# Two chained blocks on one core: norms issued one column block ahead, modulations and weight splits moved forward, and matvec chunks at three per four experts

## What is computed

```python
h = rmsnorm(x, norm1_g) * (1 + sc1) + sh1
z = h @ w_in                    # latents, conv input, gates
x = x + gt1 * ((g_attn * y_attn + g_conv * y_conv) @ w_out)
h = rmsnorm(x, norm2_g) * (1 + sc2) + sh2
x = x + gt2 * hierarchical_moe(h, ...)   # 32 experts, 4 groups of 8, top 1 group, top 2 experts
x = rmsnorm(x, final_norm_g)
# second block, layer 0 (gated delta rule) and layer 1 (softmax attention with forget gates), each:
h = rmsnorm(x, norm_w) * (1 + scale) + shift
x = x + gate * mixer(h)
```

## Time and profile before

| what | value |
|---|---|
| median of 3 runs | 1219.14 us (1217.68 to 1224.91) |
| the profiled execution | 1220.97 us |
| its span, first to last instruction | 1219.2 us |
| mean granted TensorE clock | 0.932 of full |
| PE busy | 1070.9 us, 88% |
| DVE, ACT, POOL busy | 639.4, 491.9, 398.6 us |

### The profile page before, as it was taken

How to read it: one execution, slowest core, us unless ns; L and a number is a source line. 1 busy time by engine, 2 the same in 40 slices (tenths; PEclk the granted TensorE clock), 3 DMA queues, 4 the chain that set the end, 5 groups by cost and what they waited for, 6 DMA issues and landing times.

```text
span 1219.2 us, 20059 instructions
## 1 busy us (share of the span) xinstructions
PE 1070.9 (88%) x8110; PEld 925.1 (76%) x8110; DVE 639.4 (52%) x1382; ACT 491.9 (40%) x1100; POOL 398.6 (33%) x337
## 2 busy tenths in 40 slices
PE   2589778899899999999599989999889977999986
PEld 2487567788777777776588879899779866888865
DVE  7777976374434444545554535544454434455463
ACT  2434334322211011014386756836643533565542
POOL 0551334020000000101477464455433425554431
PEclk9699989799799999999699989999989978999988
DMA  9522451577089999731222222323221213323301
GB/s 349 212 91 109 142 203 35 234 267 297 1 337 353 406 387 400 294 133 74 103 104 97 79 70 71 104 70 106 70 70 39 102 37 123 117 107 113 131 35 35
DMA packets 25724, 186.22 MB, mean 153 GB/s; under 512 B 4128, under 2 KB 4768, under 8 KB 5536
## 3 DMA queue, kind: packets, MB, share of 16 engines
q1 hardware_dynamic: 24048, 184.77, 39.8%
q10 hardware_dynamic: 432, 0.18, 0.1%
q0 software_dynamic: 1152, 0.00, 0.0%
HBM read 196.46 MB, written 1.05 MB: 162 GB/s over the span
## 4 chain that ended last, share of the span: by engine, by line
PE 70%; DVE 18%; ACT 8%; issue 3%; DMA 2%; POOL 1%; DVEq 0%; ACTq 0%; POOLq 0%; SPq 0%
PE bank L666 67%; DVE arena L2092 5%; DVE sz L2092 2%; PE bank L670 2%; DVE arena L2089 2%; ACT wH L1489 1%; DVE hT L2092 1%; ACT arena L1489 1%; ACT xH L1486 1%; DVE wL L2089 1%; ACT arena L1486 1%; DVE xL L2092 1%; DVE arena L2095 1%; ACT tmpc L1486 1%; DMA ring<-in_exw,small 1%
## 5 line engine op out<-in xcount | busy, mean ns | idle before, releaser
L2916 POOL TENSOR_TENSOR wL<-ring,wH 128x512 fp32r<-128x512 f32 x210 | 279.8, 1346 | 336.2 <-ACT wH L1489 335.7
L666 PE MATMUL bank<-xH,wH 128*128 128x256 f32 x800 | 253.7, 317 | 33.5 <-DVE xL L2092 25.6
L666 PE MATMUL bank<-xH,wL 128*128 128x256 f32 x800 | 233.4, 292 | 0.0
L666 PE MATMUL bank<-xL,wH 128*128 128x256 f32 x800 | 232.6, 291 | 0.0
L666 PEld LDWEIGHTS bank<-xH,wH 128*128 128x128 f32 x800 | 160.4, 200 | 49.5 <-issue 34.7
L666 PEld LDWEIGHTS bank<-xH,wL 128*128 128x128 f32 x800 | 161.2, 201 | 4.7 <-issue 4.3
L1489 ACT ACTIVATE wH<-ring 128x512 fp32r<-128x512 f32 x264 | 154.0, 619 | 21.5 <-DMA ring<-in_wts 12.9
L666 PEld LDWEIGHTS bank<-xL,wH 128*128 128x128 f32 x800 | 160.4, 200 | 0.0
L666 PE MATMUL bank<-ring,xg 128*128 128x256 f32 x640 | 145.3, 380 | 2.6 <-DMA ring<-in_exw,small 1.5
L666 PEld LDWEIGHTS bank<-ring,xg 128*128 128x128 f32 x640 | 119.8, 190 | 24.5 <-issue 6.0
L2092 DVE SCALAR_TENSOR_TENSOR sz<-ring,cact,sz 128x512 f32<-128x512 f32 x168 | 132.1, 786 | 5.0 <-DMA ring<-in_wts 0.3
(11 more groups left out here) (201 smaller groups left out, 1831.7 us busy)
## 6 DMA issues: line engine op xcount, KB each, us to landing
ring<-in_wts SPq DMA_DIRECT2D x123, 1024.0 KB, 4.9
ring<-in_exw SPq DMA_DIRECT2D x32, 1536.0 KB, 8.9
ring<-in_wts SPq DMA_DIRECT2D x1, 1152.0 KB, 5.3
xT<-in_xT SPq DMA_DIRECT2D x1, 1024.0 KB, 13.5
out<-hT SPq DMA_DIRECT2D x4, 256.0 KB, 2.5
cst<-in_cst SPq DMA_DIRECT2D x1, 928.5 KB, 11.7
ring<-in_wts SPq DMA_DIRECT2D x1, 640.0 KB, 3.5
vec<-in_vec SPq DMA_DIRECT2D x1, 216.5 KB, 5.5
```

The costliest lines, as they stand in the source:

```text
L666: return pe.matmul(o, l, r, start=start, stop=stop, skip_group_check=True)
L2916: return pool.tensor_tensor(o, x, h.bitcast(F32), ALU.subtract)
```

## The change

It does five things. (1) In norms 0, 2 and 3 DVE issues y one block ahead: y0, y1, l0, y2, l1, ..., y7, l6, l7; ACT and POOL keep their order. (2) `modulation(2)` moves into the expert loop at u = 30, `modulation(3)` in front of the third output projection; each waits for the last y of the norm before. (3) The splits of `gqk0a` and `gqk0b` move into the loop: ACT does two quarters at each of u = 38 to 41, DVE four turns at each of u = 40 and 41 (its own quarters are the fourth of each chunk; at u = 41 they stand behind `low_y(4)`), POOL does them when its loads are out. ACT's wait becomes: the last expert and the last matvec chunk that lie in columns 12288 to 20480, which are `ov3` and `ada2_1_4a`. (4) `fqk0b`'s splits move into norm 3, one quarter behind every second block, on ACT, DVE and POOL. (5) Matvec halves are placed at three per four experts, the last two at u = 34, and matvec steps run at 8 in 5 iterations. The ring gets fixed spots for `ov1`, `ov4`, `ov6`, and `before()` no longer stops at the first chunk that covers the start.

```diff
-        while h < 28 and 10 * h <= 7 * u:
+        while h < 28 and (4 * h <= 3 * u or u == 34):
@@ ring_spots
         k = PLACE[name][1]
+        at = {"ov1": 0, "ov4": RING, "ov6": 4096}.get(name, at)
@@ before
             out.append(ORDER[m])
-            if a <= lo:
-                break
@@
+AHEAD = [(0, "y")] + [(k + x, n) for k in range(8) for x, n in ((1, "y"), (0, "l")) if k + x < 8]
@@ the expert loops of PE and DVE
-                for _ in range((u + 1) * 7 // 5 - u * 7 // 5):
+                for _ in range((u + 1) * 8 // 5 - u * 8 // 5):
                     next(gad, None)
@@ ACT, high()
                         if name[:4] == "gqk0":
-                            e.wait_ge(dn_p, 39)
-                            e.wait_ge(ada_acc, (23, 7))
+                            for s, key in under_split():
+                                e.wait_ge(s, key)
@@ ACT, normed (POOL's normed alike)
                     fn(oh[:, k, :], hT[:, k, :], ACT.Identity, bias=shift(k)).then_inc(norm_a.up((u, k)))
+                    if u == 3 and k % 2:
+                        split.go()
@@ ACT, expert loop
+                if 38 <= u:
+                    split.go()
+                    split.go()
...
-            split.need("gqk0b")
@@ DVE
             def modulation(u, at, out_of, *gains):
                 e.wait_ge(ada_out, out_of)
+                if u:
+                    e.wait_ge(norm_d, (u - 1, 7, "y"))
...
             def normed(u, r, oh, ol, shift):
-                for k in range(8):
-                    stt(hT[:, k, :], xT[:, k, :], modA[:, k:k + 1], r, ALU.mult, ALU.mult).then_inc(norm_d.up((u, k, "y")))
-                    e.wait_ge(norm_a, (u, k))
-                    stt(ol[:, k, :], hT[:, k, :], shift(k), oh[:, k, :].bitcast(F32), ALU.add, ALU.subtract).then_inc(norm_d.up((u, k, "l")))
+                for k, n in AHEAD:
+                    if n == "y":
+                        stt(hT[:, k, :], xT[:, k, :], modA[:, k:k + 1], r, ALU.mult, ALU.mult).then_inc(norm_d.up((u, k, "y")))
+                    else:
+                        e.wait_ge(norm_a, (u, k))
+                        stt(ol[:, k, :], hT[:, k, :], shift(k), oh[:, k, :].bitcast(F32), ALU.add, ALU.subtract
+                            ).then_inc(norm_d.up((u, k, "l")))
+                        if u == 3 and k % 2:
+                            split.go()
@@ DVE, expert loop
+                if u == 30:
+                    modulation(2, 56, 15, vcol("norm_w_2", 0, 8), vcol("final_norm_g", 0, 8))
                 if 2 <= u and (u - 2) % 8 == 7:
                     low_y((u - 2) // 8)
+                if 40 <= u:
+                    for _ in range(4):
+                        split.go()
...
-            split.need("gqk0b")
-
-            modulation(2, 56, 15, vcol("norm_w_2", 0, 8), vcol("final_norm_g", 0, 8))
...
+            modulation(3, 80, 23, vcol("norm_w_2", 8, 8))
             nx = out_proj("ao", 2, 3, 64)
...
-            split.need("fqk0b")
-            modulation(3, 80, 23, vcol("norm_w_2", 8, 8))
+            split.need("fqk0a")
```

More of the change, by code:

```diff
@@ L471, in build_program @@
         r2_d = sig("r2_d", range(3))
-        norm_d = sig("norm_d", [(u, k, n) for u in G4 for k in K8 for n in ("y" if u == 1 else "yl")] + [(4, k, "y") for k in K8])
+        norm_d = sig("norm_d", [(u, k, n) for u in G4 for k, n in ([(k, "y") for k in K8] if u == 1 else AHEAD)] + [(4, k, "y") for k in K8])
         norm_a = sig("norm_a", [(u, k) for u in G4 for k in K8])
@@ L584, in ada_name, with under_split @@
             return f"ada{j}" if j < 12 else f"ada2_{j // 6 - 2}_{j % 6}"
+        def under_split():
+            names = [n for n in WIDE if SPOT[n][0] < RING and 12288 < SPOT[n][1]]
+            return [freed_by([n for n in names if (n[:3] == "ada") == x][-1])[0] for x in (False, True)]
         def used(name):
```

## The result

Slower by 0.6%, where I had forecast a little faster: median 1227.91 us (1222.02 to 1235.07, 9 runs) against 1219.24 (1217.68 to 1224.91, 9 runs), ratio 1.0064 with a 95% interval of 1.0036 to 1.0091. My number was 1217.9, the top of my range 1226.0. The profiled execution took 1229.9 us, its span is 1228.1, 8.9 more than before.

The account below looks back on a forecast made before the run. PE was taken to bound the kernel (70% of the chain of waits, busy 88%). Terms -0.9 - 5.1 - 1.2 + 6.0 = -1.2 took the median from 1219.1 to 1217.9 us; range 1213 to 1223, widened to 1208 to 1226.

Parts of the forecast that it names:

- Part 4: Expert stage: new placement, spots and matvec steps make PE stand longer, +6.0 us (4.5 to 14).
- `ada2_1_4b` +3.4: Expert stage, iteration 32: this half lands late, DVE's `hid` is late, and PE stands 3.4 us.
- `ov3` +3.0: Expert stage, up(35): the load waits for columns shared with `ov0`, and PE stands 3.0 us.
- `ov4` -1.5: Expert stage, in front of up(36): the old stall on this load goes, 1.5 us won.
- other narrow margins: Expert stage: eighth expert and matvec steps at u = 26 to 31 with barely landed halves, +1.1 us (0 to 3.4).
- Rival C: u = 20 to 34: DMA queues decide, halves land late, PE stands in several iterations; stage +12.0, total 1223.9 us; chance 0.18.
- Part 1: Norms 0, 2 and 3: y ahead leaves the beat at 1.44 us, gains only at the ends; norm 0 -0.9 us.
- rival A: Norms 0, 2, 3: DVE and POOL do not hold each other; norms' sum -15.4, total 1209.7 us; chance 0.15.
- the price of a pair of taps: DVE's taps beside POOL's `wL`: one pair per 1.41 us, taken as alternating and used for the norms' beat.
- the bound: Norms: with free engines the last l would come 4.5 us earlier, against 1.0 forecast.
- Part 2: In front of norm 2: splits and `modA` gone, y0 starts 4.8 us earlier; -5.1 us in all (-3.5 to -5.5).
- Part 3: Norm 3: first y 3.3 us earlier, POOL's three `wL` inside cost 3.1; PE reaches `forgets` 1.2 earlier (0 to 5).

Follow-up runs that it names:

- the second run: Kernel before with y one block ahead, both modulations moved and fqk0b's splits inside norm 3, expert stage's weights untouched: 1209.86 us, ratio 0.9909.

## Why the prediction was wrong, step by step

**Part 4 is the step that failed: +6.0, measured +24.2.** Its named stalls were right: `ada2_1_4b` +3.4 (3.50), `ov3` +3.0 (2.92), `ov4` -1.5 (gone). By place the excess grows by 7.6 up to `turn_hid(10)`, by 10.2 from there to `turn_hid(31)`, by 5.0 to `turn_hid(33)` and by 1.4 to the last. The last two, 6.4, hold the stalls that I had worked out, at 4.9. The first two, 17.8, stood in my sum as +1.1. (Between the parts this can be off by some 2 us, since the column sums, 0.9 a group, now come earlier.) The profiled execution is a costly one: in two other kernels with the same placement, spots and steps the stage is 20.3 and 17.4 longer than before. Three terms were missing or too small; the first lies within the other two and within the named stalls, so they are not to be added up.
- *The clock behind a stall*: costed at nothing, measured +11.1 as longer busy time. I wrote "PE stands +3.4" and stopped there; the runs with dummy work show that stalls of 3.8 and 4.8 us cost half as much again, and shorter ones can.
- *Bank 7*: I followed each step's weights and each step's place in front of `gated_up`, not what a step's result lies in until DVE fetches it. The profile of before has the wait (0.8 on `adaT` in the list of PE's waits above), and I didn't ask what the phase of the steps does to it. 4.8 us of waiting more than before, and with the clock 7.6 at the tenth `turn_hid`, of which `close()` moved gave back 6.0.
- *Late halves in the middle of the stage*: taken as +1.1 with "other narrow margins". From `turn_hid(10)` to `turn_hid(31)` the excess grows by 10.2. DVE stood for 37.6 + 33.2 = 70.8 us for `in_wts`, where it had stood for 0.3 (the waits of DVE, above). Most of that was slack of DVE's, whose wait for `silu` fell from 108.6 to 57.4; PE stood for `hid` for 7.6 in the whole stage. The cause is the one that I began with, 0.8 halves used and 0.75 placed, but I let it bite only at its last half; with 0.75 used it is gone.

Rival C had the direction and, in part, the place. It gave +12.0 for the stage, and it had the wrong mechanism: it held the denser placement to be too much for the queues, and the runs with that placement and 3 steps in 2 show no such thing. Its sign, four and more gaps from u = 20 on, is in the trace (0.50, 2.12, 0.48, 3.50 and 2.92), so that sign did not tell its mechanism from the other. That the steps run ahead of the placement through the whole stage, and that they hold a bank, was in none of my cases.

**Part 1 failed too, the other way: -0.9, -0.3 and -1.0; rival A was right.** The last l ends 8.0 us behind the first y in norm 0, and in norm 2 too (11.8 before); in norm 2 PE's last group of `decays` starts 10.0 behind it instead of 12.8. I carried the price of a pair of taps beside `wL`, a POOL instruction with two inputs and 512 columns, over to one with one input and 256. The nearer row would have been POOL's shift itself, but no row of before had y beside it, and I gave the bound too little weight. The rule of the Trainium skill that I set beside it (SBUF — State Buffer, "Who interferes with whom") would have had the second instruction blocked for the first one's whole length. Norm 3 shows nearly that (1.50 for a y beside `wL`), norm 0 shows 0.70 beside the shift; where they differ, the measurement decides. I had also run two of its sentences together: the Trainium skill says "for the whole instruction" of VectorE's two-port modes in that section, and of two inputs in SBUF that they contend. And the taps agreed less well with taking turns than I wrote: POOL's `wL` took 1.41 beside them for 1.29 alone, and a pair 0.36 less than the two in turn.

**Part 2: y0 of norm 2 4.8 earlier.** Measured from the last `turn_hid`: 18.96 against 23.89, -4.9. Right in size, but not in its halves: with the modulation alone moved (the second run) it is 22.59, so `modA` gave 1.3 and not 2.4, and moving the splits as well gave the other 3.6. Its end for PE is A's: -7.8, not -5.1.

**Part 3: -1.2.** The first y came 3.1 earlier, counted from the end of `decays` (-3.3 said). The last l is 9.8 behind it, so 1.9 less instead of the 2.1 more that I had worked out: the three `wL` cost less than their length. PE reached `forgets` 4.9 earlier, which is A's -5.0, and lost 3.4 behind it to the clock. From the end of `decays` to the end of the program nothing is left of the gain: 616.1 against 616.3.

**The starting point.** My sum was made against an execution whose first part was 4 us longer than usual: it reaches the first `turn_hid` at 333.2, while the four kernels of this study that leave norm 0 as it was do so at 327.6 to 329.0. In the twelve with y ahead it is 320.0 to 330.1, at the median 326.0. So of the -7.1 in the first part some 3 are norm 0's and about 4 that execution's own; with a spread of 10 us between traces this is rough. With the gains of A (-15.4) and the measured stage (+24.2) the sum would have been +8.8, where the medians differ by 8.7. The near agreement is luck in part: it leaves out the 4 of that first part and the +4.6 behind `forgets`, which happen to cancel.

## What to carry to other kernels

When a change speeds up the consumer of a stream, compare its rate with the supply's over the whole stage, not at the last item, and look at every resource that its results occupy (here a PSUM bank) against the fixed points of the other work: the phase of the steps alone cost 6 us here. Where PE runs at full clock, cost a stall of 4 or 5 us at one and a half times its length, and give a shorter one a range of up to 2 us more. Before reading a difference of a few us between two kernels as the edit's, look where in the trace it lies: here it lay in parts that the edit does not touch. Before carrying over the price of a contention from one pair of instructions to another, ask whether the partner has the same number of inputs and the same size, and keep the uncontended case as a real candidate.

## What the runs showed of the hardware

- DVE's y (two inputs in SBUF, 128x256) beside POOL's scalar add (one input, 128x256): 0.70 us for 0.48, POOL 1.03 for 0.93. Beside POOL's subtraction of two inputs (128x512): 1.50.
- Single-input DVE adds of 128x256 last 0.29 us each in the record and start every 0.204 us.
- PE's clock stayed at its upper level behind a stall of 2.38 us and was at its lower one behind stalls of 3.75 and 4.80, all in the kernel before with dummy adds. It was at the lower one too behind 1.54 in one of these runs and behind 2.12 in the changed kernel, and at the upper one behind 1.47 in the kernel before.
- With three weight subtractions of POOL's between the blocks of norm 3, PE's clock fell 3 to 4 us behind the start of `forgets` in eight traces of eight; without them in none of nine.
- The same program part can differ by several us from one profiled execution to another: up to the first `turn_hid` 326.0, 326.0, 322.3 and 322.4 us in four kernels that differ only behind it or in one line of DVE's order.
